# Second mixer: where ScalarE rounds the last output weights, and where VectorE puts its scans, gated inputs and remainders

## What is computed

```
def rglru_direction(uh, w_r, b_r, w_i, b_i, lam, reverse):
    r = sigmoid(u @ w_r + b_r);  i = sigmoid(u @ w_i + b_i)     # 256x256 blocks
    log_a = -RG_C * r * softplus(-lam);  a = exp(log_a)
    gated = sqrt(-expm1(2.0 * log_a)) * (i * u)
    h = scan over positions of (a, gated)                        # h_t = a_t h_(t-1) + gated_t
...
h = rglru_direction(..., reverse=False) + rglru_direction(..., reverse=True)
return (gelu(y_branch) * h) @ w_out
```

## Time and profile before

| | |
|---|---|
| median of three runs | 1837.43 us |
| the profiled execution's own time | 1836.84 us |
| its span, first to last instruction | 1835.0 us |
| mean granted TensorE clock | 0.955 |
| PE busy | 1685.0 us (92%) |
| DVE busy | 715.7 us (39%) |
| ACT busy | 511.3 us (28%) |
| chain that ended last | PE 73%, DMA 13%, DVE 7%, ACT 5% |

### The profile page before, as it was taken

One profiled execution on the slowest core, in us unless ns is written; L12 is line 12 of the kernel. 1 busy time (PEld: TensorE's weight loads), 2 busy tenths in 40 slices (PEclk: granted clock), 3 DMA queues, 4 the chain that ended last, 5 costly groups with the idle time before them and its releaser, 6 DMA issues.

```text
span 1835.0 us, 25708 instructions
## 1 busy us (share of the span) xinstructions
PE 1685.0 (92%) x10638; PEld 1146.6 (62%) x10638; DVE 715.7 (39%) x1356; ACT 511.3 (28%) x780; POOL 269.3 (15%) x165
## 2 busy tenths in 40 slices
PE   5989898999989899999999998997799999999987
PEld 2678597999989755445444446887454454443547
DVE  1566624999256512122121214657321221221223
ACT  3444335444444301111110115465211111111123
POOL 1406411577410100000000001000100000000010
PEclk9999888999999889999999998997799999999999
DMA  9203524353636559999999993433599999999960
GB/s 406 79 27 132 230 97 191 138 184 127 218 138 275 230 228 429 428 428 428 428 428 428 428 429 143 155 128 145 245 419 426 428 429 428 429 428 428 429 273 24
DMA packets 37516, 528.08 MB, mean 288 GB/s; under 512 B 4160, under 2 KB 4288, under 8 KB 4800
## 3 DMA queue, kind: packets, MB, share of 16 engines
q1 hardware_dynamic: 36864, 525.22, 69.3%
q10 hardware_dynamic: 576, 1.75, 0.3%
HBM read 525.91 MB, written 1.05 MB: 287 GB/s over the span
## 4 chain that ended last, share of the span: by engine, by line
PE 73%; DMA 13%; DVE 7%; ACT 5%; issue 1%; POOL 0%; SPq 0%; DVEq 0%; ACTq 0%
PE bank L475 23%; PE bank L944 19%; DMA ring<-in_w_up 11%; PE bank L970 10%; PE bank L901 3%; PE bank L902 3%; PE bank L544 2%; PE bank L468 2%; PE bank L917 2%; DMA ring<-in_dense 2%; PE bank L918 1%; PE bank L1046 1%; DVE ring_rounded L1630 1%; ACT work L1396 1%; PE bank L649 1%
## 5 line engine op out<-in xcount | busy, mean ns | idle before, releaser
L475 PE MATMUL bank<-xn_rounded,ring_rounded 128*128 128x256 f32 (+1 forms) x2560 | 354.4, 292 | 14.7 <-DVE xn_rounded L1620 14.2
L944 PE MATMUL bank<-ring,work 128*64 128x512 f32 x1536 | 342.5, 601 | 13.2 <-DMA ring<-in_w_up 11.0
L475 PEld LDWEIGHTS bank<-xn_rounded,ring_rounded 128*128 128x128 f32 x2560 | 329.3, 197 | 21.4 <-issue 16.8
L944 PEld LDWEIGHTS bank<-ring,work 128*64 128x64 f32 x1536 | 113.2, 139 | 236.7 <-issue 223.6
L1519 POOL TENSOR_TENSOR ring_rounded<-ring,ring_rounded 128x2048 fp32r<-128x2048 f32 (+1 forms) x43 | 187.0, 4369 | 288.8 <-ACT ring_rounded L1113 288.8
L475 PE MATMUL bank<-work_rounded,ring_rounded 128*128 128x256 f32 (+1 forms) x1232 | 190.3, 296 | 6.8 <-DVE ring_rounded L1630 3.8
L2087 DVE TENSOR_TENSOR work<-work,bank 128x512 f32<-128x512 f32 x32 | 22.0, 687 | 412.9 <-PE bank L944 412.9
L475 PEld LDWEIGHTS bank<-work_rounded,ring_rounded 128*128 128x128 f32 x1232 | 164.2, 190 | 15.4 <-DVE ring_rounded L1630 4.0
L1113 ACT ACTIVATE ring_rounded<-ring 128x2048 fp32r<-128x2048 f32 (+1 forms) x88 | 154.6, 1806 | 57.1 <-PE bank L475 35.7
L970 PE MATMUL bank<-ring,work 128*64 128x512 f32 x768 | 170.1, 595 | 0.0
L1589 POOL TENSOR_TENSOR work<-work_rounded,work 128x128 f32<-128x128 f32 x64 | 24.2, 399 | 841.9 <-PE bank L963 836.6
(11 more groups left out here) (308 smaller groups left out, 1826.0 us busy)
## 6 DMA issues: line engine op xcount, KB each, us to landing
ring<-in_dense SPq DMA_DIRECT2D x50, 2048.0 KB, 8.3
ring<-in_w_gate SPq DMA_DIRECT2D x48, 2048.0 KB, 20.2
ring<-in_w_up SPq DMA_DIRECT2D x48, 2048.0 KB, 22.1
ring<-in_w_down SPq DMA_DIRECT2D x48, 2048.0 KB, 24.9
work<-in_w_gate SPq DMA_DIRECT2D x16, 2048.0 KB, 18.9
work<-in_w_up SPq DMA_DIRECT2D x16, 2048.0 KB, 23.6
work<-in_w_down SPq DMA_DIRECT2D x16, 2048.0 KB, 27.0
ring<-in_dense SPq DMA_DIRECT2D x8, 1408.0 KB, 6.5
```

The costliest lines, as they stand in the source:

```text
L475: last = mm(out, rv(ring[r][:, at:at + P]), rv(x[part][k]), start=k == 0 and j == 0, stop=k == n_k - 1 and j == 2)
L944: last = mm(b[64 * y:64 * y + 64, :], xg[:, k, 64 * y:64 * y + 64], ws[y][:, 512 * k:512 * k + 512], start=k == 0, stop=k == KT - 1)
```

## The change

It changes orders only. On ScalarE, the rounding of chunk `w_out_b + 1` stands before the first gate function and no longer after that of `i = 4`; the first two `rounded_out` stand between the gate functions of the second half and no longer after them. On VectorE, the subtraction for that chunk follows `i = 1` instead of `i = 4`; the exponents 8 to 15, which stood in groups of 3 and 5, stand in groups of 4, 2 and 2 with `rest(0)`, `scans(2)` and `rest(1)` between; and the second half's `gated_input(1)` stands before `variances(1)` instead of behind it.

```diff
@@ ScalarE @@
         for half in range(2):
             functions(SIGMOID)
+            if half == 0:
+                split_next()
             for i in range(KT * half, KT * half + KT):
                 gate_functions(i)
-                if i == KT // 2:
-
-                    split_next()
                 if i % KT:
                     tangent(i - 1)
+                if i in (13, 14):
+                    rounded_out(i - 13)
             after(tangent(KT * half + KT - 1))
-            if half:
-                rounded_out(0)
-                rounded_out(1)
             functions(EXP)
@@ VectorE @@
             last = gated_input(i % 2, i // 2)
-            if i == KT // 2:
+            if i == 1:
                 weights_low(FIRST["w_out_b"] + 1)
         after(last)
         variances(0)
         increments(0)
         scans(0)
-        exponents((8, 9, 10))
         scans(1)
-        exponents(range(11, 16))
+        exponents(range(8, 12))
         rest(0)
         scans(2)
+        exponents((12, 13))
         rest(1)
+        exponents((14, 15))
         gated_input(0, slice(4, 8))
+        after(gated_input(1, slice(4, 8)))
         variances(1)
         rest(2)
-        after(gated_input(1, slice(4, 8)))
         scans(3)
         increments(1)
```

## The result

Over 20 runs of each, the changed kernel takes 1841.19 us (median, 1836.36 to 1845.67) and the kernel before 1837.51 us (1832.88 to 1842.15). The ratio is 1.0020, with a 95% interval of 1.0011 to 1.0029: slower by 3.7 us, and under the 0.5% that I set as the bound of "the same". The forecast was 1841.9 us.

A forecast was written before the change was run, and what follows sets the result against it. The mixer was taken to set when the experts' weight stream restarts, so its time passes on in full. +6.5 - 0.74 - 1.22 = +4.5 us on the median of 1837.43 gave 1841.9 us, range 1835.4 to 1847.5.

The forecast's parts named there:

- The span behind the mixer: From mixer to end: the experts' weight stream restarts after the mixer, so a microsecond there passes on at full price.
- rival 2: Experts' stage: the weight stream sets its own end and absorbs the change, time stays 1837.4 us; chance 0.10.
- The wait: Mixer's first half: ScalarE stands 5.57 us for the chunk's landing, then rounds 3.60 us; TensorE idles 5.6 us.
- Rival 1: Mixer's first half: the stall is hidden and only the second half's 1.96 us gain counts, 1835.5 us; chance 0.12.
- The subtraction: VectorE after tile 1: its 4.5 us fit between ScalarE's tiles and cost nothing, at most 4.5 us without that cover.
- The clock in the bursts: TensorE's four gate uses after each mixer stall: 9.69 us with the low clock; first half's table load +6.5 us.
- Rivals 3 and 4: TensorE's stalled restarts: 3, clock stays 0.50 through both bursts, 1850.3 us, chance 0.06; 4, low clock missed, 1839.2 us, chance 0.10.
- Rival 4: TensorE's new gap: the low clock is missed, first half +3.8 us, +1.8 in all, 1839.2 us; chance 0.10.
- The second half: Mixer's second half: two roundings in ScalarE's waits give -0.74 us, the gated input hidden ahead of the variances -1.22 us.

The follow-up runs named there:

- the run with the wait alone: The kernel before, with ScalarE also waiting for the chunk's landing ahead of the first gate function and rounding at the old place; ratio 1.0019.
- the run with idle work: The changed kernel with 12 unread products on TensorE ahead of gate use 4, to fill its stall; ratio to the kernel before 1.0005.
- the version cut in two: The kernel before with the second half's edits and the rounding split, after gate functions 4 and 11; ratios 0.9974 and 0.9987.
- the kernel with the first half alone: The kernel before with only the rounding ahead of the gate functions and VectorE's subtraction after tile 1; ratio 1.0038.

## Why the prediction was right

**The span behind the mixer.** From the first refill to the end it is 508.0 to 510.6 us in all eleven profiles, while the refill itself moves over 12.8 us from the stage's start. The end follows the refill, so rival 2, that the stream absorbs it, is out: the changed kernel lost 4.1 us up to the refill and 3.7 us in the medians. That the weight stream is what holds the experts' stage was not needed for this and is not shown: TensorE is busy there for 417 of 430 us, and it too starts from the mixer's end.

**The wait.** First gate function 1228.60 - 1216.85 = 11.75 us after TensorE's first product, where the prediction had 1225.4 - 1213.71 = 11.7. TensorE's stall is 5.56 us, where I had 5.6. Rival 1 is out by the stall and by the run with the wait alone. The part of it by which an earlier landing would hide the wait wasn't tried, since the slot sets the issue.

**The subtraction.** VectorE's subtraction after tile 1 cost nothing, as priced: it ran from 1230.80 to 1235.28, and the last exponent of the half was done at 1239.63, before ScalarE had its table at 1241.35.

**The clock in the bursts.** The mis-sized term, once too large and once too small. I took 9.7 us from the second half's burst, and the new one took 1238.41 - 1229.48 = 8.93. So the edit costs 5.75 and not 6.5 us. The other way round, the second burst took 10.21 and not 9.69, and the two errors cancel to 0.24. That the sum came within 0.2 us of the measured +4.34 is in part this luck. Rivals 3 and 4 lie on either side: neither burst stayed low, nor did the clock miss the stall. (Rival 4's +3.8 for the first half is close to the run with idle work, +3.9, where the clock was kept up.) Across the profiles restarts after 5.5 us and more took 8.87 to 10.21 us for the same four uses; from a single burst I could not know it better.

**The second half.** Gate function 15 to the table: 1262.64 - 1260.98 = 1.66 us against 2.40, the forecast number. To step 3 15.70, the forecast number too. The risk that I had named for it, that the exponents stand behind `rest(0)` and the scans, did not come: VectorE had both gated inputs done 1.70 us ahead of the squares.

**What I had wrong.** I gave marks in absolute time, the first gate function at 1225.4, the table near 1237.7 and the refill at 1330.7. They came at 1228.60, 1240.06 and 1333.41, since the stage itself began 3.1 us later. As times from the stage's start they would have been 11.7, 24.0 and 117.0, against 11.75, 23.21 and 116.56. And I took the clock to fall 2 us into a stall, from one gap; over the profiles' stalls of 5 us and more it took 2.0 to 4.8 us.

## What to carry to other kernels

Before an in-order engine is made to round, copy or convert a load earlier, look up when the load is issued and when it lands: everything behind it on that engine waits, and here four banks of cover were not enough for 5.6 us of wait and 3.6 us of work. Work that is movable belongs where its engine already waits for another, in pieces no larger than its waits add up to before the next thing that others wait for. Counted from the version cut in two, the same rounding made the table 7.5 us later in front and 1.8 us later in one piece in the middle, and its second piece cost nothing that shows at step 3. And measure a change of some 4 us inside its stage, from an event ahead of it to one behind, since the stage's start alone moves by 6 us between programs that are the same up to there.

## What the runs showed of the hardware

How long TensorE stands before the granted clock falls is less steady than I had read from one gap. In the changed kernel it stopped at 1223.9, and the window 1226 to 1228 above has 0.54: some 2 us. In its second stall it stopped at 1245.3, and the windows there are:

```profile
1248.00:1250.00 2.00, 0.00 (x0) 0.00 (x0) 2.00 (x2) 1.97 (x3) 0.00 (x0) 1.00 0.00 0
1250.00:1252.00 2.00, 1.23 (x3) 1.05 (x4) 1.90 (x5) 2.00 (x6) 0.00 (x0) 0.51 0.00 0
```

The clock held until 1250, more than 4.7 us, and fell 0.8 us ahead of the restart. That it fell in this stall of 5.49 us at all, as I had counted on, was closer than my 2 us made it look. Nor does a short stall protect: with the wait alone TensorE stood for 1.96 us only, and the clock fell 0.3 us after it had restarted. After the 2.82 us in front of the output product it fell in the kernel before (0.50 in the window 1254 to 1256), and it stayed at 1.00 after the same 2.82 us in the kernel with the first half alone (1257 to 1262).
